# A product with 512 moving columns in place of two with 256, in six residual projections

## The chip, the cores and the metric

One Trainium2 chip, and one of its cores. The metric is the device time of one execution, in microseconds; the program is launched once and does the whole computation.

## The reference

Three blocks on one sequence of 256 tokens and 1024 features, in float32: a Mamba2 mixer with a conv FFN; differential attention with a conv FFN; and a block that joins a sparse attention and a gated recurrence, with a third conv FFN. What matters here is how each mixer and each FFN ends. It is a projection that is added to the stream `x`:

```python
x = x + y @ out_w                       # Mamba2, 2048 -> 1024       ("so")
x = x + (silu(gate) * up) @ down_w      # FFN, 2816 -> 1024          ("dn0", "dn1")
x = x + o @ attn_out_w                  # attention, 1024 -> 1024    ("ao")
h = h + ga1 * (merged @ w_out)          # 1024 -> 1024               ("wout")
h = h + ga2 * ((silu(gte) * val) @ w_down)   # 2816 -> 1024          ("dn2")
```

After each of them stands an RMS norm of the new `x` over its features, and the next products need its result.

## The kernel before

**Precision by halves.** Every large product is made from two halves of each operand. A weight slab (128 partitions x 2048 numbers, 1 MB) lands in `raw`; ScalarE rounds it to the float32r half `wh` (`split_hi`, line 377) and VectorE forms the rest `wl = raw - wh` (`split_lo`, line 384). Activations are split in the same way into a high and a low half. One contraction step is three matmuls of 128 x 128 weights and 256 moving columns (the tokens) into one PSUM bank (`mm3`, line 579): `wl*xh`, `wh*xl`, `wh*xh`. All of them are issued on line 584. I call the three a triple below.

**Streams.** `make_plan` (line 107) numbers all slabs, PSUM groups and semaphore counts in the order of the program. Slabs go through a ring of three buffers (`RING`) and PSUM groups through six banks (`PRING`). `stream` (line 587) waits for `lo_done` of a slab, takes a free bank for each output tile of 128 features and issues the triples. A 1 MB slab holds 16 triples: in `so` one tile of 16 steps, in `ao` and `wout` two tiles of 8 steps, in `dn` (kind `PAIR3`) three slabs of 16, 16 and 12 triples make two tiles of 22 steps each. So the six projections have 128, 176, 64, 176, 64 and 176 triples (so, dn0, ao, dn1, wout, dn2), 784 of the kernel's 2808.

**Who splits when.** There is no other scheduler than the written order of each engine's own queue. In a residual stage, at step s, VectorE (lines 1411 and 1430) does: one `ada` product, `split_lo` of slab s+2, a second `ada` product, and then for each tile m that is finished in step s the residual add (lines 1418, 1420, 1444, 1446), which gives the bank back, and `accumulate` of the square of tile m-1 (line 1380). ScalarE (lines 982 and 1008) does: `split_hi` of slab s+2, and then for each finished tile the square of the new `x[:, m]` (line 990), for which it waits until the bank has been given back. `split_hi` waits for the transfer of its slab and for TensorE to be through with the slab three before it. SyncE issues the load of a slab when `split_lo` of the slab three before it is done (line 516). ScalarE's last `split_hi` of a stage stands behind the square of tile 7 and ahead of the square root of the norm.

**The ada products.** The conditioning product `silu(c) @ w_ada` of the third block has no place of its own: VectorE works on it in 96 pieces of 128 x 512 numbers (`ada`, line 1358, instruction on line 1367), spread over the slabs of earlier streams by the table `ADA` (line 209): so 5 slabs, dn0 10, ao 3, dn1 10, with two pieces for each slab; wout and dn2 have none. The pieces come through a ring of two buffers (`ARING`) with 256 KB transfers that GpSimd issues (line 561), each after VectorE has used the piece two before it.

Of the kernel before, what the change touches and what calls it, by code (L numbers as in the profile page):

```python
# [236 lines left out]
def build_program(nc, io, out):  # L237
    with ExitStack() as ctx:
# [15 lines left out]
        xh = sb("xh", [P, KD, T], F32R)  # L254
        xl = sb("xl", [P, KD, T], F32R)
# [31 lines left out]
        def R(off, a, b):  # L287
            return actr[:, off:off + a * b].rearrange("p (a b) -> p a b", b=b)

# [111 lines left out]
        hh, hl = R(0, NF, T), R(NF * T, NF, T)  # L401
# [18 lines left out]
        yh, yl = R(0, 16, T), R(16 * T, 16, T)  # L420
# [14 lines left out]
        x2h, x2l = R(0, 8, T), R(8 * T, 8, T)  # L435
        oh, ol = R(16 * T, 8, T), R(24 * T, 8, T)
# [24 lines left out]
        rh, rl = R(0, 8, T), R(8 * T, 8, T)  # L461
        ah, al = R(16 * T, 4, T), R(20 * T, 4, T)
        mh, ml = R(24 * T, 8, T), R(32 * T, 8, T)
# [114 lines left out]
        def _(pe):  # L578
            def mm3(o, w, xp, start, stop, tok):

                (w_h, w_l), (x_h, x_l) = w, xp
                for n, (a, b) in enumerate(((w_l, x_h), (w_h, x_l), (w_h, x_h))):
                    l, r = (b, a) if tok else (a, b)
                    mm = nc.tensor.matmul(o, l, r, start=start and n == 0, stop=stop and n == 2)  # L584
                return mm

            def stream(name, X, ready=None):
# [6 lines left out]
                def stage(i, j):  # L594
# [4 lines left out]
                    if kind == TWO and ready and isinstance(i, int) and i == 0 and j == 0:  # L599
# [3 lines left out]
                        for k in range(kts):  # L603
                            ready(k)
                            for t in range(2):
                                off = k * width + t * P
                                mm = mm3(bank(g0 + t)[:, 0:T], (wh[:, r, off:off + P], wl[:, r, off:off + P]),
                                         (X[0][:, k, :], X[1][:, k, :]), k == 0, k == kts - 1, False)
                                if k == kts - 1:
                                    mm.then_inc(half_done if t == 0 else slab_done, 1)  # L610
                        return
                    for t in range(tiles):
# [14 lines left out]
                        for k in ks:  # L627
# [4 lines left out]
                            wp = (wh[:, r, off:off + P], wl[:, r, off:off + P])  # L632
                            mm = mm3(bank(g)[:, 0:T], wp, (X[0][:, k, :], X[1][:, k, :]), st, en, False)
# [7 lines left out]
            def stream_tok(name, X):  # L641

                for s in range(PL.N[name]):
# [3 lines left out]
                    for t in range(2):  # L647
                        g = PL.G[name] + 2 * s + t
                        acquire(pe, g)
                        for k in range(KD):  # L650
                            mm = mm3(bank(g)[:, 0:256],
                                     (wh[:, r, k * 256:k * 256 + 256], wl[:, r, k * 256:k * 256 + 256]),
                                     (X[0][:, k, P * t:P * t + P], X[1][:, k, P * t:P * t + P]),
                                     k == 0, k == KD - 1, True)
# [48 lines left out]
            stream("xbc", (xh, xl), x_ready(0))  # L703
# [58 lines left out]
            for gr in range(4):  # L762
                stream(f"za{gr}", (xh, xl))
# [8 lines left out]
                stream(f"zb{gr}", (xh, xl))  # L772
# [13 lines left out]
            stream("so", (yh, yl), lambda k: pe.wait_ge(low_done, k + 1))  # L786

            def ffn(f, norm, use, r):
                norm_sum(norm, r)
                stream(f"up{f}", (xh, xl), x_ready(use))  # L790
                stream(f"dn{f}", (hh, hl), lambda k: pe.wait_ge(low_done, LOW0 + NF * f + k + 1))
# [65 lines left out]
            for s in range(6):  # L857
                if s < 4:
                    stream(f"k{s}", (xh, xl), x_ready(2) if s == 0 else None)
# [6 lines left out]
                if s < 4:  # L866
                    stream(f"q{s}", (x2h, x2l), x_ready(3) if s == 0 else None)
                if 1 <= s < 5:
                    scores(2 * s - 1)
                if s < 4:  # L870
                    sums_by_token("kss", s, k_squares, halves)
                    stream_tok(f"v{s}", (xh, xl))
# [8 lines left out]
            stream("ao", (oh, ol), lambda k: pe.wait_ge(ol_done, k + 1))  # L881
# [12 lines left out]
            stream("qb", (xh, xl), x_ready(5))  # L894
            stream("kk", (xh, xl))
# [5 lines left out]
            for k in range(KD):  # L901
                o = k * 256
                mm = mm3(bank(g)[:, 0:T], (wh[:, b % RING, o:o + P], wl[:, b % RING, o:o + P]),
                         (xh[:, k, :], xl[:, k, :]), k == 0, k == KD - 1, False)
            mm.then_inc(half_done, 1)
            for c in range(2):
                for k in range(KD):
                    o = k * 256 + P
                    mm = mm3(bank(g + 1)[:, P * c:P * c + P], (wh[:, b % RING, o:o + P], wl[:, b % RING, o:o + P]),
                             (xh[:, k, P * c:P * c + P], xl[:, k, P * c:P * c + P]), k == 0, k == KD - 1, True)  # L910
            mm.then_inc(slab_done, 1)
            stream("qi", (xh, xl))
# [25 lines left out]
            for s in range(4):  # L938
                stream(f"yr{s}", (xh, xl))
                if s:  # L940
                    gates(s - 1)
                stream(f"xr{s}", (xh, xl))
            for it in range(9):
                if it < 8:
                    stream(f"{'ga' if it < 4 else 'gb'}{it%4}", (xh, xl))
# [20 lines left out]
            stream("woa", (ah, al), lambda k: pe.wait_ge(al_done, k + 1))  # L966
            pe.wait_ge(rl_done, 8)
            stream("wor", (rh, rl))
            stream("wout", (mh, ml), lambda k: pe.wait_ge(ml_done, k + 1))
# [377 lines left out]
        def _(dve):  # L1347
# [62 lines left out]

            def residual(name, r, n, tiles, scale=None):
                for s in range(n):
                    if s < n - 1:
                        lo(name, s)
                    for m, g, t, cnt in tiles(s):
                        wait_tile(dve, name, s // RING, s % RING, t, cnt)
                        if scale is None:
                            ins = V.tensor_tensor(x[:, m, :], bank(g)[:, 0:T], x[:, m, :], ALU.add)
                        else:
                            ins = V.scalar_tensor_tensor(x[:, m, :], bank(g)[:, 0:T], scale(m), x[:, m, :],  # L1420
# [695 lines left out]
```

## Time and profile before

| | |
|---|---|
| time, median of 3 runs | 1367.28 us (1366.11 to 1369.92) |
| span of the profiled execution, first to last instruction | 1370.0 us |
| TensorE (matmul) busy | 1218.9 us, 89% |
| VectorE busy | 936.6 us, 68% |
| ScalarE busy | 721.9 us, 53% |
| chain that ended last | PE 65%, DVE 15%, ACT 9%, DMA 6% |
| bytes read from HBM | 214.3 MB, 159 GB/s over the span |

The profile gives the span of its execution, not its device time; the span is 2.7 us over the median of the runs and 0.1 us over the slowest of them. The page names engines PE (TensorE), PEld (its weight loads), DVE (VectorE), ACT (ScalarE), POOL (GpSimd) and SP (SyncE). In a timeline, a row is one instruction or several alike that follow each other: start, time, engine, line, output<-inputs, shape, count, and in brackets how long the engine had been idle before it and what released it. Matmuls overlap, so what one costs in a dense stretch is the distance between starts and not its own duration.

### The profile page before, as it was taken

Reading aid. Unit: us, or ns where it says so; the run is one execution under the profiler, and the core shown is the slowest. Engines: PE = TensorE matmul, PEld = TensorE weight load, DVE = VectorE, ACT = ScalarE, POOL = GpSimd, SP = SyncE. Lnnn points to the kernel's source line nnn. Section 1 sums busy time; section 2 is a strip of 40 time slices with the busy share of each in tenths; the row PEclk is TensorE's granted clock in tenths of the full one; section 3 lists DMA queues with packets and bytes.
Section 4 is the critical chain, followed back from the end, with each engine's and each line's share of the span. In section 5 each row is a group of like instructions: output and inputs, shape, how many; then the busy total and the mean of one; then the engine's idle time right before and its main releaser. Section 6 shows DMA issues by size and latency. Waiting matters only on the chain.

```text
span 1370.0 us, 24509 instructions
## 1 busy us (share of the span) xinstructions
PE 1218.9 (89%) x9392; PEld 1183.2 (86%) x9392; DVE 936.6 (68%) x1699; ACT 721.9 (53%) x1078; POOL 56.6 (4%) x115
## 2 busy tenths in 40 slices
PE   4868989889999989886899999899777899999997
PEld 3868888889999988885899999898766788999997
DVE  4557778768787677665588877637865556888753
ACT  4354556446666336555366663446684434766641
POOL 1000000010000111010000001000000000000000
PEclk9988989999999999896899999889998989999998
DMA  6564422365554756442345557554322344455550
GB/s 236 126 186 154 133 99 100 129 233 181 181 181 163 261 200 223 139 144 80 139 158 183 183 177 265 186 185 133 130 93 78 123 154 154 158 182 183 175 192 32
DMA packets 38936, 219.62 MB, mean 160 GB/s; under 512 B 4775, under 2 KB 9160, under 8 KB 17352
## 3 DMA queue, kind: packets, MB, share of 16 engines
q1 hardware_dynamic: 26296, 185.83, 39.4%
q0 software_dynamic: 8112, 26.75, 5.6%
q10 hardware_dynamic: 4448, 5.94, 2.3%
q8 instruction: 55, 0.90, 0.3%
q14 instruction: 25, 0.20, 0.0%
HBM read 214.30 MB, written 4.19 MB: 159 GB/s over the span
## 4 chain that ended last, share of the span: by engine, by line
PE 65%; DVE 15%; ACT 9%; DMA 6%; issue 3%; ACTq 1%; SPq 0%; DVEq 0%
PE ps L584 58%; DMA raw<-in_xbc 4%; DVE wl L384 4%; ACT wh L377 3%; DMA ada_w<-in_w_ada 2%; PE ps L745 1%; DVE ada_w L1367 1%; DVE work L1399 1%; PE ps L671 1%; PE ps L756 1%; ACTq L1041 1%; DVE small L1743 1%; DVE work L1625 1%; DVE xl L1393 1%; DVE work L1874 1%
## 5 line engine op out<-in xcount | busy, mean ns | idle before, releaser
L584 PE MATMUL ps<-xh,wl 128*128 128x256 f32 x1784 | 520.0, 292 | 28.3 <-DVE wl L384 18.2
L584 PE MATMUL ps<-xl,wh 128*128 128x256 f32 x1784 | 515.0, 289 | 0.0
L584 PE MATMUL ps<-xh,wh 128*128 128x256 f32 x1784 | 514.4, 288 | 0.0
L384 DVE TENSOR_TENSOR wl<-raw,wh 128x2048 fp32r<-128x2048 f32 (+1 forms) x178 | 400.8, 2254 | 152.0 <-ACT wh L377 152.0
L584 PEld LDWEIGHTS ps<-xh,wl 128*128 128x128 f32 x1784 | 353.6, 198 | 34.2 <-DVE wl L384 19.1
L377 ACT ACTIVATE wh<-raw 128x2048 fp32r<-128x2048 f32 (+1 forms) x178 | 333.7, 1877 | 83.8 <-PE ps L584 55.2
L584 PEld LDWEIGHTS ps<-xl,wh 128*128 128x128 f32 x1784 | 353.3, 198 | 0.5 <-issue 0.2
L584 PEld LDWEIGHTS ps<-xh,wh 128*128 128x128 f32 x1784 | 353.0, 198 | 0.0
L584 PE MATMUL ps<-actr,wh 128*128 128x256 f32 x1888 | 342.8, 284 | 0.0
L584 PEld LDWEIGHTS ps<-actr,wh 128*128 128x128 f32 x1888 | 296.8, 193 | 0.1
L584 PE MATMUL ps<-actr,wl 128*128 128x256 f32 x944 | 270.2, 286 | 3.2 <-DVE wl L384 2.0
L584 PEld LDWEIGHTS ps<-actr,wl 128*128 128x128 f32 x944 | 182.7, 194 | 5.9 <-DVE wl L384 3.0
L1509 DVE SCALAR_TENSOR_TENSOR work<-ps,vecs,work 128x255 f32<-128x255 f32 (+1 forms) x336 | 143.8, 475 | 45.0 <-ACT work L1152 41.6
L1152 ACT ACTIVATE work<-ps,vecs 128x256 f32<-128x256 f32 x132 | 74.3, 565 | 140.9 <-PE ps L584 140.7
L990 ACT ACTIVATE work<-x 128x256 f32<-128x256 f32 x56 | 22.4, 416 | 132.2 <-DVE x L1444 37.6
L1367 DVE CUSTOM_DVE_ANT_0 ada_w<-ada_w,cact 128x512 f32<-128x512 f32 x96 | 65.3, 686 | 36.3 <-DMA ada_w<-in_w_ada 36.1
L561 POOL DMA_DIRECT2D ada_w<-in_w_ada x96 | 51.9, 541 | 814.8 <-DVE ada_sum L1367 814.0
L1185 ACT ACTIVATE work<-work,small 128x128 f32<-128x128 f32 (+1 forms) x48 | 21.5, 448 | 30.1 <-DVE small L1743 30.1
L1006 ACT ACTIVATE xh<-work 128x256 fp32r<-128x256 f32 x48 | 19.9, 417 | 19.0 <-DVE work L1399 18.5
L661 PEld LDWEIGHTS ps<-tri,work 128*128 128x128 f32 x60 | 9.9, 241 | 23.1 <-issue 23.1
L661 PE MATMUL ps<-tri,work 128*128 128x1 f32 x60 | 10.1, 282 | 22.1 <-DVE work L1380 22.1
L1143 ACT ACTIVATE work<-work 128x256 f32<-128x256 f32 x66 | 26.7, 404 | 2.9 <-DVE work L1509 2.8
(240 smaller groups left out, 1098.5 us busy)
## 6 DMA issues: line engine op xcount, KB each, us to landing
raw<-in_up SPq DMA_DIRECT2D x66, 1024.0 KB, 4.9
ada_w<-in_w_ada POOLq DMA_DIRECT2D x96, 256.0 KB, 4.4
raw<-in_xbc SPq DMA_DIRECT2D x12, 1024.0 KB, 16.1
raw<-in_z SPq DMA_DIRECT2D x8, 1024.0 KB, 4.9
raw<-in_so SPq DMA_DIRECT2D x8, 1024.0 KB, 5.1
raw<-in_dn0a SPq DMA_DIRECT2D x8, 1024.0 KB, 5.4
raw<-in_dn1a SPq DMA_DIRECT2D x8, 1024.0 KB, 5.3
raw<-in_dn2a SPq DMA_DIRECT2D x8, 1024.0 KB, 4.9
```

Source lines behind the costliest of these rows:

```text
L377: nc.scalar.activation(wh[:, b % RING, 0:n], raw[:, b % RING, 0:n], ACT.Copy).then_inc(hi_done, 1)
L384: nc.vector.tensor_tensor(wl[:, b % RING, 0:n], raw[:, b % RING, 0:n], wh[:, b % RING, 0:n].bitcast(F32), ALU.subtract).then_inc(lo_done, 1)
L561: pool.dma_start(ada_w[:, a % ARING, :], io["w_ada"][a // 2][:, 512 * (a % 2):512 * (a % 2) + 512])\
L584: mm = nc.tensor.matmul(o, l, r, start=start and n == 0, stop=stop and n == 2)
L661: mm = nc.tensor.matmul(o[:, n * b_:n * b_ + n], tile[:, P * b_:P * b_ + P], cols, start=True, stop=True)
L990: A(sq[:, m % 2, :], x[:, m, :], ACT.Square).then_inc(sq_done, 1)
L1006: A(xo[:, m, :], xn[:, m, :], ACT.Copy).then_inc(xh_done, 1)
L1143: A(gsil[:, (j - 1) % RING, :], pre[:, 2 * ((j - 1) % RING), :], ACT.Silu)\
L1152: A(pre[:, 2 * (j % RING) + t, :], bank(tile_group(up, j, t))[:, 0:T], ACT.Identity, scale=vdyn(f"up_w{f}", 88 + 2 * s + t), bias=vdyn(f"u ...
L1185: A(lg[:, cols], lg[:, cols], ACT.Exp, scale=-1.0, bias=mins[:, q, row + i:row + i + 1], accum_out=sums_[:, row + i:row + i + 1]).then_inc ...
L1367: V.tensor_tensor_reduce(out=w, in0=w, in1=cact[:, 512 * half:512 * half + 512], scale=1.0, scalar=0.0, op0=ALU.mult, op1=ALU.add, accum_o ...
L1509: return V.scalar_tensor_tensor(dst[:, d:T], src[:, 0:T - d], w, dst[:, d:T], ALU.mult, ALU.add)
```

## The change

The two halves of each operand become slices of one tensor, so that both halves of a moving tile can be named in one access (`xhl`, `yhl`, `hhl`, `ohl`, `mhl` and so on; the addresses inside are those of before). In the six residual projections the triple becomes two matmuls: `wh` against high and low half together, 512 moving columns, into both halves of the bank, and `wl` against the high half, 256 columns, into the first half of the bank. The residual then adds the two halves of the bank one after the other, with a wait on VectorE's own step counter between them. All other streams keep their three matmuls in the same order.

```diff
-        wh = sb("wh", [P, RING, SLOT], F32R)
-        wl = sb("wl", [P, RING, SLOT], F32R)
+        whl = sb("whl", [P, 2, RING, SLOT], F32R)
+        wh, wl = whl[:, 0, :, :], whl[:, 1, :, :]
...
+            def mm2(o, r, cols, X, k, start, stop):
+
+                nc.tensor.matmul(o, wh[:, r, cols], X[:, :, k, :], start=start, stop=False)
+                return nc.tensor.matmul(o[:, 0:T], wl[:, r, cols], X[:, 0, k, :], start=False, stop=stop)
...
-            def stream(name, X, ready=None):
+            def stream(name, X, ready=None, halved=False):
...
-                            wp = (wh[:, r, off:off + P], wl[:, r, off:off + P])
-                            mm = mm3(bank(g)[:, 0:T], wp, (X[0][:, k, :], X[1][:, k, :]), st, en, False)
+                            if halved:
+                                mm = mm2(bank(g), r, slice(off, off + P), X, k, st, en)
+                            else:
+                                mm = mm3(bank(g)[:, 0:T], r, slice(off, off + P), X, k, st, en)
...
-            stream("so", (yh, yl), lambda k: pe.wait_ge(low_done, k + 1))
+            stream("so", yhl, lambda k: pe.wait_ge(low_done, k + 1), halved=True)
...
-                stream(f"dn{f}", (hh, hl), lambda k: pe.wait_ge(low_done, LOW0 + NF * f + k + 1))
+                stream(f"dn{f}", hhl, lambda k: pe.wait_ge(low_done, LOW0 + NF * f + k + 1), halved=True)
...
-            stream("ao", (oh, ol), lambda k: pe.wait_ge(ol_done, k + 1))
+            stream("ao", ohl, lambda k: pe.wait_ge(ol_done, k + 1), halved=True)
...
-            stream("wout", (mh, ml), lambda k: pe.wait_ge(ml_done, k + 1))
+            stream("wout", mhl, lambda k: pe.wait_ge(ml_done, k + 1), halved=True)
...
+            def add_halves(m, g, scale):
+
+                for half in range(2):
+                    part = bank(g)[:, T * half:T * half + T]
+                    if half:
+                        step.wait()
+                    if scale is None:
+                        ins = V.tensor_tensor(x[:, m, :], part, x[:, m, :], ALU.add)
+                    else:
+                        ins = V.scalar_tensor_tensor(x[:, m, :], part, scale(m), x[:, m, :], ALU.mult, ALU.add)
+                    if half:
+                        give_back(ins, g)
+                    else:
+                        step.add(ins)
```

Both `residual` and `residual3` call `add_halves` where they had the one add.

## Rows read from the trace of the kernel before

**Rows 1.** The page, parts 1 and 4 (busy time; shares of the chain).
```profile
PE 1218.9 (89%) x9392; PEld 1183.2 (86%) x9392; DVE 936.6 (68%) x1699; ACT 721.9 (53%) x1078; POOL 56.6 (4%) x115
...
PE 65%; DVE 15%; ACT 9%; DMA 6%; issue 3%; ACTq 1%; SPq 0%; DVEq 0%
```

**Rows 2.** Busy time by window; columns PE, PEld, DVE, ACT, POOL, clock, DMA share, GB/s.
```profile
261.00:303.00 42.00, 39.93 (x326) 39.05 (x324) 28.51 (x55) 16.36 (x16) 5.38 (x10) 1.00 0.69 237
437.00:501.00 64.00, 63.63 (x531) 63.43 (x529) 43.04 (x72) 24.62 (x24) 10.76 (x20) 1.00 0.74 253
657.50:682.00 24.50, 24.27 (x193) 24.07 (x192) 16.27 (x31) 8.96 (x13) 3.23 (x6) 0.95 0.56 194
816.00:880.00 64.00, 63.37 (x529) 63.16 (x527) 43.15 (x72) 24.76 (x25) 9.68 (x18) 1.00 0.74 252
1137.00:1160.50 23.50, 22.91 (x191) 22.71 (x190) 14.63 (x24) 10.58 (x15) 0.00 (x0) 1.00 0.52 178
1296.00:1359.60 63.60, 63.04 (x526) 62.83 (x524) 28.37 (x30) 22.74 (x24) 0.00 (x0) 1.00 0.35 119
1200.00:1250.00 50.00, 50.00 (x419) 50.00 (x418) 40.30 (x60) 29.78 (x45) 0.00 (x0) 1.00 0.53 180
```

**Rows 3.** TensorE timeline: start, us, engine, line, instruction, count.
```profile
175.99 1.89 PE L725 MATMUL ps<-work,tri 128*128 128x256 f32 x8
...
657.67 0.63 PE L584 MATMUL ps<-actr,wh 128*128 128x256 f32 x2
...
917.80 0.28 PE L584 MATMUL ps<-wh,xl 128*128 128x128 f32 x1
...
918.81 0.27 PE L584 MATMUL ps<-wh,xl 128*128 128x128 f32 x1
```

**Rows 4.** The chain that ended last, end of so: start, us, what.
```profile
286.01 5.31 DMA ada_w<-in_w_ada
...
292.04 0.35 DVE x L1418
...
292.73 1.91 ACT wh L377
...
294.67 2.30 DVE wl L384
...
297.01 6.03 PE ps L584 x48
```

**Rows 5.** VectorE timeline: six dependent small instructions ahead of so; the last add of so.
```profile
261.30 1.18 DVE L1468 SCALAR_TENSOR_TENSOR small<-small 128x8 f32<-128x8 f32 x6
...
303.06 0.42 DVE L1418 TENSOR_TENSOR x<-ps,x 128x256 f32<-128x256 f32 x1 [0.53 <-PE ps L584]
```

**Rows 6.** VectorE timeline, ends of dn0 and dn1.
```profile
492.88 1.76 DVE L384 TENSOR_TENSOR wl<-raw,wh 128x1536 fp32r<-128x1536 f32 x1 [0.92 <-ACT wh L377]
...
500.67 0.42 DVE L1444 TENSOR_TENSOR x<-ps,x 128x256 f32<-128x256 f32 x1 [1.31 <-PE ps L584]
...
868.81 0.69 DVE L1367 CUSTOM_DVE_ANT_0 ada_w<-ada_w,cact 128x512 f32<-128x512 f32 x1 [3.40 <-DMA ada_w<-in_w_ada]
...
872.37 1.76 DVE L384 TENSOR_TENSOR wl<-raw,wh 128x1536 fp32r<-128x1536 f32 x1 [0.92 <-ACT wh L377]
...
879.40 0.42 DVE L1444 TENSOR_TENSOR x<-ps,x 128x256 f32<-128x256 f32 x1 [1.40 <-PE ps L584]
```

**Rows 7.** VectorE timeline, wout.
```profile
1153.86 2.29 DVE L384 TENSOR_TENSOR wl<-raw,wh 128x2048 fp32r<-128x2048 f32 x1 [1.71 <-ACT wh L377]
...
1159.95 0.48 DVE L1420 SCALAR_TENSOR_TENSOR x<-ps,small,x 128x256 f32<-128x256 f32 x1 [1.61 <-PE ps L584]
```

**Rows 8.** VectorE timeline, last two adds of ao; one split in dn2.
```profile
678.93 0.42 DVE L1418 TENSOR_TENSOR x<-ps,x 128x256 f32<-128x256 f32 x1 [1.22 <-PE ps L584]
...
681.81 0.42 DVE L1418 TENSOR_TENSOR x<-ps,x 128x256 f32<-128x256 f32 x1 [2.12 <-PE ps L584]
...
1325.09 2.29 DVE L384 TENSOR_TENSOR wl<-raw,wh 128x2048 fp32r<-128x2048 f32 x1 [3.47 <-ACT wh L377]
```

More of the change, by code:

```diff
@@ L288, in R, with RR @@
             return actr[:, off:off + a * b].rearrange("p (a b) -> p a b", b=b)
+        def RR(off, a, b):
+            return actr[:, off:off + 2 * a * b].rearrange("p (h a b) -> p h a b", h=2, b=b)
         KB = 256
@@ L578, in _, with mm3, mm3_tok @@
         def _(pe):
[L579 to L585, printed above, removed]
-            def stream(name, X, ready=None):
+            def mm3(o, r, cols, X, k, start, stop):
+                nc.tensor.matmul(o, wl[:, r, cols], X[:, 0, k, :], start=start, stop=False)
+                nc.tensor.matmul(o, wh[:, r, cols], X[:, 1, k, :], start=False, stop=False)
+                return nc.tensor.matmul(o, wh[:, r, cols], X[:, 0, k, :], start=False, stop=stop)
+            def mm2(o, r, cols, X, k, start, stop):
+                nc.tensor.matmul(o, wh[:, r, cols], X[:, :, k, :], start=start, stop=False)
+                return nc.tensor.matmul(o[:, 0:T], wl[:, r, cols], X[:, 0, k, :], start=False, stop=stop)
+            def mm3_tok(o, r, cols, X, k, toks, start, stop):
+                nc.tensor.matmul(o, X[:, 0, k, toks], wl[:, r, cols], start=start, stop=False)
+                nc.tensor.matmul(o, X[:, 1, k, toks], wh[:, r, cols], start=False, stop=False)
+                return nc.tensor.matmul(o, X[:, 0, k, toks], wh[:, r, cols], start=False, stop=stop)
+            def stream(name, X, ready=None, halved=False):
                 n, kind = PL.N[name], PL.kind[name]
@@ L606, in stage @@
                                 off = k * width + t * P
[L607 to L608 removed]
+                                cols = slice(off, off + P)
+                                if halved:
+                                    mm = mm2(bank(g0 + t), r, cols, X, k, k == 0, k == kts - 1)
+                                else:
+                                    mm = mm3(bank(g0 + t)[:, 0:T], r, cols, X, k, k == 0, k == kts - 1)
                                 if k == kts - 1:
@@ L1416, in residual @@
                         wait_tile(dve, name, s // RING, s % RING, t, cnt)
[L1417 to L1420, printed above, removed]
-                                                         ALU.mult, ALU.add)
-                        give_back(ins, g)
+                        add_halves(m, g, scale)
                         if m:
```

74 lines of the change are left out of this document (36 added, 38 removed).

## The prediction, made before the kernel with the change had run

> **What bounds the kernel now.** I read the shares first. TensorE's matmuls are busy 89% of the span and hold 65% of the chain that ended last [rows 1], so a change that takes time off matmuls looks right. But that is a mean over stages, and only six stages change. So the next view is the busy time of each of these [rows 2]: in dn0, dn1 and dn2 TensorE is busy over 99% of the window, in ao and wout 97 to 99%, in so 95%. Third, what a matmul costs: in a dense stretch 419 start in 50 us, one every 0.12 us, a triple in 0.36 us [rows 2], where the array needs 256 columns at 2.4 GHz, 0.107 us. Fourth, and this decides, for each stage the work that feeds TensorE and the work between its last matmul and the next stage: the chain and the timelines of VectorE [rows 4 to 8].
>
> **What a triple will cost.** Removed: one matmul of 256 columns and its weight load. Doubled: the columns of another. The trace has no float32r matmul of 512 columns. The nearest row is a float32 one of 256 columns, which shows as two records for each matmul and streams 512 array cycles in each: eight records in 1.89 us, the last lasting 0.38, so (1.89 - 0.38) / 7 = 0.216 us apart [rows 3]. That is 512 columns at 2.4 GHz (0.213) and almost nothing more, so the 0.013 us that today's matmul costs beyond its columns is not paid per column there. With half the columns (128) the distance is 0.112 (nine steps from 917.80 to 918.81) [rows 3]; so a floor near 0.11 per weight load holds short matmuls up, and a 512-column one covers it. I take 0.216 for the long one and leave 0.120 for the short one: 0.336 us for a triple in place of 0.360. Bounds: 0.360 if the long one costs twice 0.120, nothing gained; 0.325 if the short one falls to 0.109. Where the clock is at its lower level (1.2 GHz) matmuls stand 0.63 - 0.41 = 0.22 us apart [rows 3], which is all columns, and the change gives nothing; ao's mean clock of 0.95 over 24.5 us [rows 2] means 2.5 us at the lower level, its first four triples.
> The Trainium skill ("TensorE: Matmul & The Clock Gate", Back-to-back issue gap) gives a warm gap of N/2.4 + 2.5 ns: 109 for 256 columns, 216 for 512. By it a triple would cost 328 now and 325 after, and the change would have nothing to win. The long matmul's row agrees with it, the short one's (120) does not.
> At 24 ns for each of 784 triples the most to be had is 18.8 us: so 3.1, dn 4.2 each, ao and wout 1.5 each. What follows is how much of it each stage can use.
>
> **What the residual costs.** For each of 8 tiles in 6 stages VectorE runs a second add that waits for the first. An add takes 0.42 us (0.48 where it scales) [rows 6, 7], and a dependent instruction starts 0.03 us after its forerunner's end (six of 0.17 us in 1.18) [rows 5]. So each tile costs 0.45, in wout and dn2 0.51 us. The bank comes free that much later, and ScalarE's square waits for it; behind the square in ScalarE's queue stands the next `split_hi`, for which VectorE's `split_lo` waits, for which TensorE waits. Six banks cover the bank itself. Whether the loop is covered is a question for each stage. (The saved weight loads and the order `wh` before `wl` cost nothing, since both halves are there when `lo_done` lets TensorE start.)
>
> *so.* The chain does not run over matmuls here: it goes ada transfer (5.31 us), add, `split_hi`, `split_lo`, and TensorE starts the last slab at 297.01, right when its `split_lo` ends (294.67 + 2.30) [rows 4]. Faster matmuls are worth nothing, since each slab waits for its split. The extra adds are on this loop, except where an ada transfer hides one: tiles 1, 2 and 4, 3 x 0.45 = 1.35 us to the last slab. After it come tiles 5, 6 and 7 with one more `split_hi` and `split_lo` between them, another 1.35, less the 0.53 us for which VectorE waited for tile 7 [rows 5]. Sum: +2.2 us.
> *wout.* VectorE waits for `split_hi` before every split (1.71 us before the last), and only 1.61 us for TensorE before the last add [rows 7]. Loop: `split_hi`, `split_lo`, two tiles, square, next `split_hi`. Seven extra adds ahead of tile 7 are 3.6 us; the 1.61 us swallow part, tile 7's own second half comes on top: 8 x 0.51 - 1.6 = +2.4 us. TensorE is done 1.5 us earlier and waits.
> *ao.* The same loop, but VectorE waits 1.22 us for TensorE before tile 6 and 2.12 us before tile 7 [rows 8]: seven adds are 3.2, less 1.2 and some 0.4 at the first tiles, are +1.6 and stay under 2.12. Tile 7's first half starts 0.5 earlier (TensorE is through 1.5 earlier), its second costs 0.45: 0 to -0.2, I take -0.2 us. Price without that cover: +2.
> *dn2.* No ada products. VectorE sits idle 3.47 us before a split, for `split_hi`, which waits for TensorE [rows 8]: everything is fed early, a tile needs 22 triples and the adds fall beside them. 176 x 0.024 = 4.2 saved, tile 7's second half 0.51 exposed: -3.7 us.
> *dn0 and dn1.* TensorE looks just as full [rows 2], but the cover is nearly used up. dn1's last slab (36 matmuls, 4.3 us) starts at about 879.3 - 4.3 = 875.0, and its `split_lo` ends at 872.37 + 1.76 = 874.1: 0.9 us of slack; dn0: 500.6 - 4.3 = 496.3 against 494.64, 1.6 us [rows 6]. What delays the split is an ada piece: VectorE stood idle 3.40 us for its transfer at 868.81 [rows 6], then came two adds, squares, `split_hi`, `split_lo`. The DMA engines are at 0.74 with 252 GB/s in both stages, 0.35 and 119 in dn2 [rows 2]. Each transfer is issued when VectorE used the piece two earlier, so this is a loop of its own that a faster TensorE does not shorten. With the same transfers, the last split of dn1 comes 2 x 0.45 later (875.0) and the slab takes 4.0 instead of 4.3: end at 879.1, plus 0.45, is +0.3; dn0 in the same way -0.5. The adds of tiles 0 to 3 delay the issue of later pieces by up to 0.9 each time, partly hidden under transfers; I put +0.6 on each stage for it. dn0 +0.1, dn1 +0.9. Bounds for each: -3.7 (transfers never the limit) to +2.5 (every added pair lands on the loop).
>
> **Sum.** +2.2 + 2.4 - 0.2 - 3.7 + 0.1 + 0.9 = +1.7 us. The span was 1370.0 and the median of the runs is 1367.3, 2.7 us lower; I add the sum to the median: 1369.0 us. The runs before spread over 3.8 us, so what a measurement can tell from no change is about 0.3%, 4.1 us. A longer idle time between stages can also move where the clock falls and rises; I give it no price, the runs' spread contains it. The forecast is no measurable change: 18.8 us of matmul time saved on paper, one stage that cashes it.
>
> **Rivals.**
> 1. *The long matmul costs twice the short one* (0.240). For: no row shows float32r with 512 columns, and today's price is 0.013 over the columns in every dense stretch. Against: 0.216 in the float32 row. It decides in dn2, which then has +0.5 instead of -3.7; the others hardly move. Total +5.9, 1373.2 us: slower, by the second adds alone. Chance 0.13.
> 2. *The ada loop takes the adds in full.* In dn0 and dn1, at the add pairs of slabs 2, 5 and 8, each 0.9 us later issue of pieces, with none hidden: +2.5 for each stage. It decides from the point where a piece's landing after such a pair sets the next split, as at 868.81. Total +5.7, 1373.0 us. Chance 0.10.
> 3. *The ada loop gives way.* Slab loads start earlier with a faster TensorE and the pieces land in better gaps; for it speaks that DMA is at 0.74 and not full. Then dn0 and dn1 each give up to -3.7: total -6.7, 1360.6 us, faster. Against it: VectorE's idle time before pieces, up to 3.40 us [rows 6]. Chance 0.12.
> 4. *The short matmul gets cheaper behind a long one* (0.325 for a triple, the skill's gap for both): only dn2 can use it, 176 x 0.011 = 1.9 more, total -0.2, 1367.1 us. Chance 0.15.
> The forecast itself has 0.50; about 0.05 of that lies beyond 0.3% on the slow side and 0.01 on the fast one.
>
> **Numbers.** Faster: rival 3 without its weaker half and the forecast's edge, 0.12. Slower: rivals 1 and 2 and the edge, 0.28. Same: 0.60. The range holds the forecast, rival 4 and all but the ends of the others: 1362.5 to 1374.
>
> **What would show it.** dn2: 176 triples in 59.1 us instead of 63.4, its last add 3.7 us earlier against its first matmul. so and wout: TensorE idle before slabs on `wl`, and VectorE no longer waiting for TensorE ahead of the last add. dn1: TensorE waits for `split_lo` of its last slab. Wrong would be: long matmuls not 0.216 apart; so or wout no longer than before; dn0 and dn1 each 3 us shorter.

## The result and the profile after

The kernel with the change took 1377.4 us (median of 5 runs, 1371.94 to 1379.46), the kernel before, measured beside it, 1366.11 (1365.31 to 1369.92). The ratio is 1.0067, with a 95% interval of 1.0049 to 1.0085: **some 9 us slower** (the two medians stand 11.3 apart), where no change was forecast (1369.0 us, range 1362.5 to 1374.0). The profiled execution took 1378.39 us, its span is 1376.7, 6.7 more than the span before. The span is 1.7 us less than the time of its own execution, so the execution traced before took about 1371.7 us (an estimate), more than any run of its table; the two spans therefore differ by less than the times.

The page after, its first line, the busy shares, the shares of the chain, and one of its groups (out<-in, count, busy us, mean ns, idle time before):

```profile
span 1376.7 us, 22989 instructions
...
PE 1212.3 (88%) x8608; PEld 1137.3 (83%) x8608; DVE 956.6 (69%) x1747; ACT 722.3 (52%) x1078; POOL 56.4 (4%) x115
...
PE 52%; DVE 21%; ACT 12%; DMA 9%; issue 5%; ACTq 1%; SPq 0%; DVEq 0%
...
L1009 ACT ACTIVATE work<-x 128x256 f32<-128x256 f32 x56 | 23.2, 417 | 154.1 <-DVE x L1437 85.2
```

784 matmuls are gone (9392 to 8608), and TensorE's share of the chain falls from 65% [rows 1] to 52%, while VectorE, ScalarE and DMA take 42% in place of 30%. What ends late now is what feeds TensorE. Line 1437 holds the pair of adds of a tile (line 1439 where they scale); ScalarE's squares (L1009) spend 85.2 us of their waiting on L1437, where it was 71.7 us on the single adds of the same stages (37.6 on L1444 and 34.1 on L1418). The same six stages by window, in the order of [rows 2] without its last row:

```profile
260.70:302.70 42.00, 37.25 (x204) 30.80 (x202) 30.53 (x51) 14.38 (x15) 5.37 (x10) 1.00 0.65 223
436.40:500.40 64.00, 61.74 (x351) 53.30 (x350) 44.95 (x77) 24.28 (x23) 10.73 (x20) 1.00 0.71 243
657.60:682.10 24.50, 23.54 (x129) 20.26 (x128) 19.37 (x39) 9.15 (x13) 3.22 (x6) 0.95 0.56 186
816.10:880.10 64.00, 61.15 (x342) 52.57 (x341) 43.93 (x74) 24.16 (x23) 9.66 (x18) 0.99 0.68 235
1140.50:1164.00 23.50, 22.57 (x128) 19.31 (x126) 15.93 (x26) 9.83 (x12) 0.00 (x0) 1.00 0.43 143
1302.20:1365.80 63.60, 62.23 (x353) 53.72 (x351) 32.65 (x39) 23.40 (x24) 0.00 (x0) 1.00 0.36 120
...
877.20:882.00 4.80, 4.80 (x19) 4.15 (x20) 3.93 (x6) 0.42 (x1) 0.00 (x0) 0.65 0.80 261
```

TensorE was busy for 39.93 of 42 us in so, now for 37.25; in dn1 63.37 of 64, now 61.15. The last row is the last slab of dn1: a mean granted clock of 0.65, so most of it at the lower level (1.2 GHz), where [rows 2] have 1.00 for all of dn1.

**By stage.** From the TensorE timelines of both traces, each stage from its first matmul to the next stage's first (dn2: to its last add):

```
stage   before   after   difference   forecast
so       56.6     58.0      +1.4        +2.2 (with 0.5 more in up0's first slabs: +1.9)
dn0      69.5     70.7      +1.2        +0.1
ao       30.4     30.4       0.0        -0.2
dn1      79.3     83.5      +4.2        +0.9
wout     29.3     32.2      +3.0        +2.4
dn2      64.0     63.4      -0.65       -3.7
```

With +1.9 for so they sum to +9.7. The other stretches, whose code is the same, came out 3.0 shorter in this one execution, 2.6 of them ahead of so. From so's first matmul to the end it took 1117.6 us before and 1126.9 after, 9.3 more, which is what the ratio says (9.2).

One of those stretches is longer: the norm behind dn2, with its small matmuls (L661 and L671 before, L681 and L691 after). TensorE at the end of the kernel, before, then after:

```profile
1360.62 0.58 PE L661 MATMUL ps<-tri,work 128*128 128x1 f32 x4 [1.58 <-DVE work L1380]
1361.84 0.68 PE L671 MATMUL ps<-ident,small 128*128 128x128 f32 x4 [0.64 <-DVE small L1386]
...
1366.53 0.82 PE L681 MATMUL ps<-tri,work 128*128 128x1 f32 x4 [2.10 <-DVE work L1399]
1367.99 1.19 PE L691 MATMUL ps<-ident,small 128*128 128x128 f32 x4 [0.64 <-DVE small L1405]
```

TensorE has been idle for 2.10 us in place of 1.58, and the mean granted clock of the norm is 0.66 (1365.5 to 1369.2) instead of 1.00 (1359.6 to 1362.6). From dn2's last add to the end it took 11.20 us and not 10.44, so the 0.65 that dn2 saved is gone again. In wout the last add came 2.5 us later after the stage's first matmul (26.19 us against 23.72), and the other 0.5 of its +3.0 is the norm again: its second group took 1.19 us instead of 0.68. Such a half microsecond needs no change, though: the trace of the kernel before without the ada pieces (below) has it behind wout, too, and behind dn0 the norm came out 0.5 shorter with the change (5.00 against 5.51 from the last add to the next slab). The 0.75 behind dn2 stands in both profiles of the change and in none of the kernel before.

**The long matmul.** TensorE's timeline in dn2, start, us, instruction (answers to [rows 3]):

```profile
1355.08 0.40 PE L595 MATMUL ps<-actr,whl 128*128 128x512 f32 x1
1355.31 0.28 PE L596 MATMUL ps<-actr,whl 128*128 128x256 f32 x1
1355.43 0.40 PE L595 MATMUL ps<-actr,whl 128*128 128x512 f32 x1
...
1359.67 0.40 PE L595 MATMUL ps<-actr,whl 128*128 128x512 f32 x1
```

Twelve triples in 4.24 us, so 0.353 each (forecast 0.336, before 0.360): over all of dn2 the long matmul stands 0.236 ahead of the short one and not 0.216, and the short one 0.117 ahead of the next long one. 784 triples save 5.3 us on paper instead of 18.8.

**so and wout.** ScalarE and VectorE at the end of so, then of wout (answers to [rows 4, 5, 7]; in brackets the idle time before and what ended it):

```profile
294.98 0.88 DVE L1437 TENSOR_TENSOR x<-ps,x 128x256 f32<-128x256 f32 x2
...
295.89 0.42 ACT L1009 ACTIVATE work<-x 128x256 f32<-128x256 f32 x1 [3.15 <-DVE x L1437]
296.21 1.90 ACT L381 ACTIVATE whl<-raw 128x2048 fp32r<-128x2048 f32 x1
298.15 2.29 DVE L388 TENSOR_TENSOR whl<-raw,whl 128x2048 fp32r<-128x2048 f32 x1 [1.96 <-ACT whl L381]
...
1157.29 0.42 ACT L1009 ACTIVATE work<-x 128x256 f32<-128x256 f32 x1 [0.44 <-DVE x L1439]
1157.61 1.90 ACT L381 ACTIVATE whl<-raw 128x2048 fp32r<-128x2048 f32 x1
1159.55 2.29 DVE L388 TENSOR_TENSOR whl<-raw,whl 128x2048 fp32r<-128x2048 f32 x1 [1.96 <-ACT whl L381]
1161.76 1.00 DVE L1439 SCALAR_TENSOR_TENSOR x<-ps,small,x 128x256 f32<-128x256 f32 x2
```

This is the loop of the prediction: two adds (0.88, or 1.00 where they scale), the square, only then `split_hi`, for which VectorE waits 1.96 us, then `split_lo`. In wout VectorE waited 1.61 us for TensorE before the last add [rows 7]; now nothing stands there but the adds themselves.

**dn1.** The chain that ended last, through the end of dn1 (start, us, what):

```profile
860.31 4.41 DMA ada_w<-in_w_ada
...
865.74 5.12 DMA ada_w<-in_w_ada
...
870.89 0.69 DVE ada_w L1386
...
873.09 0.44 DVE x L1437
...
873.55 0.02 ACT work L1009
...
873.87 1.48 ACT whl L381
...
875.38 1.77 DVE whl L388
...
881.29 0.21 PE ps L596
881.51 0.43 PE ps L595
```

In [rows 6] the piece before dn1's last split was taken at 868.81, 53.0 us after the stage's first matmul; now it is 870.89, 54.9 us. Behind it come two tiles' adds, two squares, `split_hi` and `split_lo`. TensorE's timeline around the start of the last slab:

```profile
874.59 0.28 PE L596 MATMUL ps<-actr,whl 128*128 128x256 f32 x1
877.19 0.50 PE L595 MATMUL ps<-actr,whl 128*128 128x512 f32 x1 [2.33 <-DVE whl L388]
```

It idles 2.33 us, and then its pairs stand 0.64 us apart (0.21 + 0.43, the chain's last two lines; 768 columns at 1.2 GHz) instead of 0.353: the last slab takes 5.73 us to its last matmul, 1.6 more than twelve triples take at the full clock (4.12).

**dn0, ao, dn2** (VectorE, answers to [rows 6, 8]):

```profile
490.51 0.69 DVE L1386 CUSTOM_DVE_ANT_0 ada_w<-ada_w,cact 128x512 f32<-128x512 f32 x1 [4.25 <-DMA ada_w<-in_w_ada]
...
681.46 0.88 DVE L1437 TENSOR_TENSOR x<-ps,x 128x256 f32<-128x256 f32 x2
...
1364.47 1.00 DVE L1439 SCALAR_TENSOR_TENSOR x<-ps,small,x 128x256 f32<-128x256 f32 x2 [0.78 <-PE ps L596]
```

dn0 waits for a piece as dn1 does. In ao the last pair of adds follows without a wait: the 2.12 us of [rows 8] are used up, and no more than that. In dn2 the last pair takes 0.52 more than the single add did.

### The profile page after: what moved, and what is told of

The parts are those of the page before. It is cut to its first block, busy times and chain, and to the rows that moved or that the text cites. A ratio compares the mean times of both kernels' runs of the same rounds, so it can differ in the third digit from the quotient of the medians.

```text
span 1376.7 us, 22989 instructions
## 1 busy us (share of the span) xinstructions
PE 1212.3 (88%) x8608; PEld 1137.3 (83%) x8608; DVE 956.6 (69%) x1747; ACT 722.3 (52%) x1078; POOL 56.4 (4%) x115
## 4 chain that ended last, share of the span: by engine, by line
PE 52%; DVE 21%; ACT 12%; DMA 9%; issue 5%; ACTq 1%; SPq 0%; DVEq 0%
PE ps L589 13%; PE ps L591 13%; PE ps L590 13%; DVE whl L388 6%; DMA ada_w<-in_w_ada 5%; ACT whl L381 5%; PE ps L595 5%; DMA raw<-in_xbc 4%; PE ps L596 2%; DVE ada_w L1386 2%; DVE x L1437 1%; DVE work L1418 1%; PE ps L691 1%; PE ps L765 1%; PE ps L776 1%
## 5 line engine op out<-in xcount | busy, mean ns | idle before, releaser
L589 PE MATMUL ps<-xhl,whl 128*128 128x256 f32 x1784 | 519.6, 291 | 29.7 <-DVE whl L388 19.6
L590 PE MATMUL ps<-xhl,whl 128*128 128x256 f32 x1784 | 514.2, 288 | 0.0
L591 PE MATMUL ps<-xhl,whl 128*128 128x256 f32 x1784 | 513.8, 288 | 0.0
L388 DVE TENSOR_TENSOR whl<-raw,whl 128x2048 fp32r<-128x2048 f32 (+1 forms) x178 | 400.9, 2254 | 151.2 <-ACT whl L381 151.1
L589 PEld LDWEIGHTS ps<-xhl,whl 128*128 128x128 f32 x1784 | 353.2, 198 | 35.7 <-DVE whl L388 20.6
L381 ACT ACTIVATE whl<-raw 128x2048 fp32r<-128x2048 f32 (+1 forms) x178 | 333.3, 1877 | 69.5 <-PE ps L596 27.8
L590 PEld LDWEIGHTS ps<-xhl,whl 128*128 128x128 f32 x1784 | 352.9, 198 | 0.5 <-issue 0.2
L591 PEld LDWEIGHTS ps<-xhl,whl 128*128 128x128 f32 x1784 | 352.1, 197 | 0.0
L595 PE MATMUL ps<-actr,whl 128*128 128x512 f32 x784 | 281.4, 403 | 8.4 <-DVE whl L388 8.0
L596 PE MATMUL ps<-actr,whl 128*128 128x256 f32 x784 | 221.0, 282 | 0.0
L595 PEld LDWEIGHTS ps<-actr,whl 128*128 128x128 f32 x784 | 148.9, 190 | 48.2 <-DVE whl L388 11.0
L596 PEld LDWEIGHTS ps<-actr,whl 128*128 128x128 f32 x784 | 149.5, 191 | 0.1
L1009 ACT ACTIVATE work<-x 128x256 f32<-128x256 f32 x56 | 23.2, 417 | 154.1 <-DVE x L1437 85.2
L589 PE MATMUL ps<-actr,whl 128*128 128x256 f32 x160 | 46.4, 290 | 1.2 <-DVE actr L1412 1.2
L590 PE MATMUL ps<-actr,whl 128*128 128x256 f32 x160 | 45.8, 286 | 0.0
L591 PE MATMUL ps<-actr,whl 128*128 128x256 f32 x160 | 45.8, 286 | 0.0
L681 PE MATMUL ps<-tri,work 128*128 128x1 f32 x60 | 10.9, 295 | 27.7 <-DVE work L1399 27.7
```

Source lines behind the costliest of these rows:

```text
L381: nc.scalar.activation(wh[:, b % RING, 0:n], raw[:, b % RING, 0:n], ACT.Copy).then_inc(hi_done, 1)
L388: nc.vector.tensor_tensor(wl[:, b % RING, 0:n], raw[:, b % RING, 0:n], wh[:, b % RING, 0:n].bitcast(F32), ALU.subtract).then_inc(lo_done, 1)
L589: nc.tensor.matmul(o, wl[:, r, cols], X[:, 0, k, :], start=start, stop=False)
L590: nc.tensor.matmul(o, wh[:, r, cols], X[:, 1, k, :], start=False, stop=False)
L591: return nc.tensor.matmul(o, wh[:, r, cols], X[:, 0, k, :], start=False, stop=stop)
L595: nc.tensor.matmul(o, wh[:, r, cols], X[:, :, k, :], start=start, stop=False)
```

## The experiments

Each ratio is to the kernel before, run beside it on the same chip (medians of 1367.7 to 1368.6 us there), with its 95% interval.

### The two halves of the change, each alone

```
# e1: matmuls of the change, one add       # e2: three matmuls of 256, two adds
-  for half in range(2):                   -  mm = mm2(bank(g), ...)
+  for half in (1,):                       +  mm = mm3(bank(g)[:, 0:T], ...)
+    part = bank(g)[:, 0:T]                +    part = bank(g)[:, 0:T]   # both times
     ...                                        ...
```

> The matmuls of the change, but a single add for each tile (it takes the first half of the bank; the second half, the product with the low part of the activations, is left out of the result). Theory A (two causes add up: a triple saves only 0.007 us instead of 0.024, and the second adds sit on a loop over VectorE and ScalarE in so, wout, dn0 and dn1): without the second adds the kernel is faster than before by what dn2, dn1, dn0 and ao can use of 0.007 us for each triple, 1 to 4 us: 1362 to 1365 us. Theory B (the matmuls themselves do the harm: TensorE is through earlier, waits, and its clock falls after the idle time, as in the last slab of dn1): 1368 us or more, and dn1's last slab again takes 5.7 us.

Measured: 1366.3 us, ratio 0.9981 (0.9966 to 0.9995). Theory A expected 1 to 4 us less than before, and the matmuls alone do help, by 2.6 us (its 1362 to 1365 us are missed, since the kernel before ran at 1368.6 here). But stage by stage it is not smooth: dn2 gives -1.2, so -1.2, dn1 -1.7 (the stretch behind it, up to wout, came out 1.6 longer), and dn0 loses 3.7. The execution traced was the slowest of the ten, 1369.82 us, so the loss in dn0 may well be larger than in most. The timeline of VectorE and TensorE at the end of dn0:

```profile
488.34 0.69 DVE L1386 CUSTOM_DVE_ANT_0 ada_w<-ada_w,cact 128x512 f32<-128x512 f32 x1 [4.56 <-DMA ada_w<-in_w_ada]
...
493.71 0.50 PE L595 MATMUL ps<-actr,whl 128*128 128x512 f32 x1 [2.83 <-DVE whl L388]
```

and the window of its last slab (columns as in [rows 2]):

```profile
493.00:500.00 7.00, 6.01 (x24) 4.94 (x24) 4.47 (x7) 1.09 (x2) 0.54 (x1) 0.76 0.89 317
```

VectorE idle for 4.56 us ahead of a piece, TensorE for 2.83, then a clock of 0.76: what happened in dn1 with the change happens in dn0 without a single added add. Theory B is right about one thing, the clock fell behind this wait, but the matmuls are not the loss: with them alone the kernel is faster.

> The three matmuls of 256 columns as before the change, with the change's two adds for each tile (both take the first half of the bank, so the stage's result is added twice). Theory A: so +2.2, wout +3.5, dn0 +1.3, dn1 +2.5 to +4, ao +0.5, dn2 +0.5: 10.5 to 12 us over the kernel before, 1376.5 to 1378.5 us, about the time of the change itself. Theory B (matmuls and the clock do it): half of that or less, 1367 to 1372 us.

Measured: 1376.76 us, ratio 1.0062 (1.0038 to 1.0085): nearly all of the change's 1.0067. By stage: so +1.7 and up0's first slabs +0.4, dn0 +1.9, ao +0.6, wout +3.0, dn1 -0.1. So the adds are the loss; the saved matmuls give little of it back. It is 8.5 us over the kernel before, less than theory A's 10.5 to 12. For dn1 theory A said +2.5 to +4, and this execution shows nothing there; up1 and the stretch behind dn1, up to wout, whose code is the same, were 1.4 longer each. The two halves add up to 5.9 us and the change to 9.2; with intervals of 2 to 3 us on each of the three, that gap isn't clear of the noise.

### Without the ada pieces of dn0 and dn1

```
-  ..., "so": 5, "dn0": 10, ... "ao": 3, "dn1": 10}
+  ..., "so": 5,            ... "ao": 3}
-  for a in range(96):       # POOL issues the pieces
+  for a in range(56):
```

> The change, without the 40 ada pieces of dn0 and dn1 (their transfers and products are left out, and so the modulation of the second block is incomplete). Theory A (in dn0 and dn1 the adds land on the loop of the ada pieces): both stages then behave like dn2, each 0.7 us shorter than the same stage of the kernel before without those pieces; the difference to that kernel is then so +2, wout +3, dn2 -0.7, dn0 -0.7, dn1 -0.7, ao 0: +3 us. Theory C (dn0 and dn1 lose for another reason, such as VectorE's own work or the clock): the difference to that kernel stays at 8 to 11 us.

> The kernel before without the same 40 ada pieces: the base for the run above. TensorE is busy over 99% of dn0 and dn1 there, so both theories expect little: 0 to -2 us against the kernel before, 1364 to 1366 us.

Measured: 1.0023 (1.0009 to 1.0037) for the change and 0.9992 (0.9975 to 1.0008) for the kernel before, both without the pieces: 0.31% apart, 4.2 us, where with the pieces it is 9.2. Between the two traces dn0 differs by -0.8, dn1 by -0.7, dn2 by -1.2 to its last matmul (-0.65 to its last add), so by +3.1, wout by +2.5. The stretches behind dn0 (up to ao) and behind dn1 (up to wout) differ by +0.9 and +0.6, so it isn't clear that what dn0 and dn1 save reaches the end. In dn1 of the change without pieces VectorE waits for TensorE before the adds of tile 6:

```profile
873.40 0.88 DVE L1437 TENSOR_TENSOR x<-ps,x 128x256 f32<-128x256 f32 x2 [3.48 <-PE ps L596]
```

With the pieces gone, TensorE never waits there and the change is no loss in any of the three dn stages. That is theory A's result, and 8 to 11 us (theory C) did not come. The run takes away the products on VectorE as well as the transfers, 20 of 0.69 us in each stage, so it doesn't tell these two apart by itself; that it is the transfer is read from VectorE's idle time for it before the last split (4.25 us in dn0 with the change, 4.56 in the run above). The pieces cost the kernel before nothing that its times show.

### The price of the long matmul

Ten groups of matmuls behind the kernel's last one (`cols(i)` stands for a block of 128 columns that changes with each i), as

```
+  for i in range(32):
+      nc.tensor.matmul(pt[:, 0, :], whl[:, 0, i % 2, cols(i)], xhl[:, :, i % 6, :], ...)
+      nc.tensor.matmul(pt[:, 0, 0:T], whl[:, 1, i % 2, cols(i)], xhl[:, 0, i % 6, :], ...)
```

> The change with ten groups of matmuls put behind its last one, into two banks that nothing reads: 96 and 64 of 256 columns; 32 long ones (512 columns) whose two halves lie 8 KB apart; 32 long ones of 512 adjacent columns; then pairs of a long and a short one: halves 8 KB apart, 22 KB apart, adjacent, and with the short one in the other bank; the three of 256; and 16 times each long-short-short and long-long-short. Theory P (every matmul pays some 0.011 us beyond its columns, long or short, and the pair pays once less than the triple): long alone 0.225 apart, a pair 0.345 to 0.353, the same for halves 8 KB, 22 KB apart and adjacent. Theory Q (a long one from two separate runs of columns pays for the jump between them): adjacent columns give 0.216 for the long one and 0.336 for the pair, separate ones 0.235 and 0.353. Theory R (the long one pays for its columns twice what the short one pays, 0.240, and the short one is cheaper behind it): long alone 0.240 wherever its columns lie.

The run took 1478.69 us; the added matmuls fill the last 108 of them, the first ones still at the lower clock. The timeline of TensorE (L995 short alone, L997 long alone with separate halves, L999 long alone with adjacent columns, L1004 pairs with the halves 22 KB apart, L1007 pairs with adjacent columns; of pairs the long one's lines):

```profile
1384.84 0.88 PE L995 MATMUL pt<-xhl,whl 128*128 128x256 f32 x6
...
1389.82 1.52 PE L997 MATMUL pt<-xhl,whl 128*128 128x512 f32 x6
...
1396.62 1.98 PE L999 MATMUL pt<-xhl,whl 128*128 128x512 f32 x8
...
1415.68 0.40 PE L1004 MATMUL pt<-actr,whl 128*128 128x512 f32 x1
...
1418.15 0.40 PE L1004 MATMUL pt<-actr,whl 128*128 128x512 f32 x1
...
1426.63 0.40 PE L1007 MATMUL pt<-xhl,whl 128*128 128x512 f32 x1
...
1429.10 0.40 PE L1007 MATMUL pt<-xhl,whl 128*128 128x512 f32 x1
```

Short: (0.88 - 0.28) / 5 = 0.120 apart. Long: (1.52 - 0.39) / 5 = 0.226, adjacent (1.98 - 0.39) / 7 = 0.227. Seven pairs from 1415.68 to 1418.15 and from 1426.63 to 1429.10: 0.353 each in both; the pairs with halves 8 KB apart and those with the short one in another bank have it too. So where the columns lie makes no difference (theory Q falls), and the long one is not twice the short one (R falls). Theory P is nearest: 512 columns at 2.4 GHz are 0.213, 256 are 0.107, and both cost 0.013 more. A pair would be 0.346 by that; it is 0.353. Over whole groups the triple of short ones takes 0.360, as before; long-short-short 0.468, nearly the sum of its parts (0.226 + 2 x 0.120 = 0.466); long-long-short 0.585, 0.013 more than its parts (0.572). Why a pair costs 0.007 more than its parts is not explained.

### ScalarE's split ahead of the squares

```
 def residual(name, r, n, last_of):
+    hi(name, 0)
     for s in range(n):
-        if s < n - 1:
-            hi(name, s)
+        if s + 1 < n - 1:
+            hi(name, s + 1)
         for m, g in last_of(s):
             square(r, m, g)
```

> The change, with ScalarE's next `split_hi` moved ahead of the squares of the tile before it, in all six stages. Theory A (the second adds cost so and wout time because the next `split_hi` stands behind the square, which waits for both adds): so and wout get back what they lost and some of what the kernel before already spent there: so -2 to -4, wout -3 to -5, dn0 and dn1 -0 to -4, against the change: 5 to 9 us below it, 1367 to 1371 us. Theory D (VectorE's own queue is the limit: two adds, an accumulation and the split for each slab): less than 2 us below the change.

> The kernel before with the same move of `split_hi`. Theory A: so -1 to -2, wout -1 to -2 (it waits less, TensorE was nearly full there), 1364 to 1366 us; so the move is worth more to the change than to the kernel before, and the two end within 3 us of each other. Theory D: no difference, 1367 to 1369 us.

Measured: 1367.49 us, 0.9993 (0.9983 to 1.0004) for the change and 0.9988 (0.9973 to 1.0002) for the kernel before; again, in more rounds:

> The kernel before with `split_hi` ahead of the squares, again, in more rounds and on one chip with the three above: 0.9988 of the kernel before (0.9975 to 0.9995).

0.9991 (0.9980 to 1.0003), as expected. The move gives the change its 9 us back; for the kernel before the times show 1.2 to 1.6 us, with intervals that just reach 1, and the two traces -1.8 us in so. With the move the change loses nothing in so (-1.6 against the kernel before, where that one with the move has -1.8), 0.6 instead of 3.0 in wout; of that 0.6 the last add is 0.1, the rest the norm at the lower clock. The kernel before gained nothing in wout by the move, where theory A had put -1 to -2. ScalarE and VectorE in wout of the change with the move:

```profile
1142.31 1.92 ACT L381 ACTIVATE whl<-raw 128x2048 fp32r<-128x2048 f32 x1 [0.91 <-PE ps L596]
...
1153.55 1.00 DVE L1440 SCALAR_TENSOR_TENSOR x<-ps,small,x 128x256 f32<-128x256 f32 x2 [1.48 <-PE ps L596]
```

`split_hi` now waits for TensorE alone, and the adds run beside it; before the last pair VectorE waits for TensorE again (1.48). Theory D falls: VectorE has time for the second adds, as long as nothing stands behind them.

### VectorE's split ahead of the ada pieces

```
 def lo(name, s):
-    ada(name, s)
     split_lo(dve, PL.S[name] + s + LEAD)
     ada(name, s)
+    ada(name, s)
```

> The change, with VectorE's `split_lo` ahead of both ada pieces of its slab in place of between them (in every stage with pieces). Theory A (in dn0 and dn1 the last slab's split stands behind a piece whose transfer is late): dn1 -3 to -4 us and dn0 -1 us against the change, so gains too, since its last split stands behind a piece as well (up to -2): 4 to 7 us below the change, 1370 to 1373 us. Theory E (what delays the last split is `split_hi` behind the adds and squares, the pieces lie beside it): less than 1.5 us below the change.

Measured: 1391.05 us, 1.0155 (1.0127 to 1.0184) of the kernel before, by the two ratios 12 us *slower* than the change (1.0067). Both theories missed. VectorE, and the issues on POOL, in dn1:

```profile
858.31 0.69 DVE L1386 CUSTOM_DVE_ANT_0 ada_w<-ada_w,cact 128x512 f32<-128x512 f32 x1 [2.67 <-DMA ada_w<-in_w_ada]
...
858.96 0.69 DVE L1386 CUSTOM_DVE_ANT_0 ada_w<-ada_w,cact 128x512 f32<-128x512 f32 x1
859.31 1.18 POOL L569 DMA_DIRECT2D ada_w<-in_w_ada  x2 [5.04 <-DVE ada_sum L1386]
...
859.58 2.29 DVE L388 TENSOR_TENSOR whl<-raw,whl 128x2048 fp32r<-128x2048 f32 x1
863.33 0.69 DVE L1386 CUSTOM_DVE_ANT_0 ada_w<-ada_w,cact 128x512 f32<-128x512 f32 x1 [1.47 <-DMA ada_w<-in_w_ada]
```

There are two buffers. With both pieces used back to back, both are free at the same time, both transfers go out together (x2), and VectorE stands idle for each pair. Pieces on either side of a split leave each transfer half a slab more. This shows the loop from the other side: in dn0 and dn1 the time from the use of a piece to the landing of the next in its buffer is what paces VectorE. Against the kernel before dn0 lost 5.5 us, dn1 5.2, and the stretch between dn0 and ao, which has pieces too, 4.0.

### The change again, and versions that use the wide matmul in fewer stages

> The change once more, nothing edited, for a second profile of it. Theory A: so (with the start of up0) +1.5 to +2.5, wout +3, dn2 -1.2, the same as in its first profile, since each of their slabs waits for the same splits; dn0 and dn1 may come out anywhere from -1.2 to +4 each, depending on whether the last slab's split waits for an ada piece for 1 us or for 3. Whole: 1.004 to 1.008 times the kernel before. If so or wout differ by over 1 us between the two profiles, the account by stages is not to be trusted.

Measured: 1.0074 (1.0055 to 1.0094). Between its trace and that of before: so and up0's first slabs +2.0, wout +3.0, dn2 -1.2 to its last matmul (-0.65 to its last add), as expected; dn0 +2.3, dn1 +4.35. From so's first matmul to the end it is +10.0. By TensorE's timeline dn0's last slab waited 1.79 us for its split, then took 5.73 us; in the change's first profile it had waited 2.26 and took 4.15. `h1_matmul_bench` has the change's own code up to the end of dn2, so its trace is a third profile of that part: dn0 +2.2 (a wait of 2.13 us, then 4.15 us for the slab), dn1 only +1.2 (a wait of 1.31, then 4.22). Of the eight waits of 1.8 us or more before a last slab in dn0 or dn1 (two in this profile and two in the change's first, one in `h1`, one in `e1`, and 3.01 and 3.83 us in `k3`) six were followed by a slab of 5.71 to 5.75 us; the two that were not are 2.13 and 2.26 us. How long the wait was does not decide it alone.

```
+ halved = name in ("dn0", "dn1", "dn2", "ao")     # m2: name in ("dn2",)
```

> The wide matmul and its second add in dn0, dn1, dn2 and ao alone; so and wout as in the kernel before; `split_hi` moved ahead of the squares in all six. Theory A: so and wout as in the kernel before with the early split (0 to -1.5 us), dn2's matmuls -1.2 and its second add +0.5, dn0 and dn1 -1 to +1 each: 1 to 2 us below the kernel before with the early split, 0.997 to 0.998 of the kernel before. Rival: the ada loop takes what dn0 and dn1 save, and the result is that of the early split alone (0.9988).

> The same, with the wide matmul in dn2 alone, the one stage without ada pieces and with its splits ahead. Theory A: 0.7 us below the kernel before with the early split, too little to be told from it by the times (0.998 to 0.9985 of the kernel before), visible in the trace as dn2's last slab 1.2 us earlier.

Measured: 0.9994 (0.9979 to 1.0010) with four stages, 0.9986 (0.9973 to 0.9999) with dn2 alone; the early split without any wide matmul had 0.9991 beside them. The three can't be told apart. Against the trace of the early split alone, four stages give dn0 -1.0, dn1 -0.1, ao -0.3, dn2 -1.2 to its last matmul, but +0.9 in the stretch behind dn0 and +0.5 behind wout's last add: the 1 to 2 us that theory A had put below the early split did not come. dn2 alone gives -1.17 to its last matmul and nothing anywhere else, which is 176 triples by 0.0067; to its last add 0.65 of it is left. Of these three the version with dn2 alone is the only one whose interval lies below 1, by less than 2 us.

## Why the prediction was wrong, step by step

**Right.** *so* (+2.2 forecast, +1.9), *wout* (+2.4, and its last add came 2.5 later) and *ao* (-0.2, 0.0): read from who waits for whom behind the square, and shown by the move of `split_hi`, which takes these losses away. The price of an added add, 0.45 and 0.51 us, is what the pairs show (0.88 for two against 0.42, 1.00 against 0.48). That the saved matmul time is worth nothing in so isn't shown: with the matmuls alone so came out 1.2 shorter, but without the pieces of dn0 and dn1, which changes nothing in so, the kernel before had it 1.0 shorter as well. In wout 1.61 us of VectorE's waiting were to swallow part of the adds, and they did. Two details were off there: TensorE is through 0.4 us earlier and not 1.5, and it is never idle ahead of a slab of wout. The 0.5 us by which the stage as a whole came out above that is the norm at the lower clock.

**Wrong: the long matmul, "I take 0.216".** It measured 0.236 ahead of a short one (0.226 alone). The row it was taken from, float32 of 256 columns in two records each, showed almost no cost beyond the columns; float32r pays 0.013 for a long matmul as for a short one, and the change between both another 0.007. So the 0.013 is not a floor of the weight load that 512 columns cover, as the prediction argued from the 128-column rows. A triple is 0.353 and not 0.336. The term was *dn2*, -3.7: it became -0.65, 3.0 us of the miss. Rival 1 named this term, with 0.240 and +0.5 for dn2; the truth lies between, nearer to it, though the long one alone is not twice the short one. The formula of the Trainium skill that was weighed there ("TensorE: Matmul & The Clock Gate", Back-to-back issue gap) puts the long one at 216 ns. The trace disagrees (236), as it did for the short one (120 against 109); but what follows from it, a triple that saves 3 ns, was closer to the 7 measured than the forecast's 24.

**Wrong: "I put +0.6 on each stage for it"**, the later issue of ada pieces in *dn0 and dn1*. The piece ahead of dn1's last split came 54.9 us into the stage and not 53.0: 2.0 us, over three times the 0.6. The second term, 0.9 for the two pairs of adds behind it, was right, and so, nearly, was the slack of 0.9, which the two used up. What had no term is what came behind TensorE's idle time of 2.33 us: a last slab with a granted clock of 0.65 over 4.8 us, 1.6 us more. Put together, 0.3 with 2.0 in place of 0.6, with 0.1 for a slab of 4.12 and not 4.0, and with 1.6 for the clock make 4.0 of the 4.2. The text said that "a longer idle time between stages can also move where the clock falls and rises; I give it no price": it fell inside a stage, and in the norm behind dn2 as well (+0.75). Rival 2 named this loop, with a bound of +2.5 for each stage; dn1 took +4.2, +4.35 and +1.2 in three profiles, dn0 +1.2, +2.3 and +2.2. The bound was too low for the first two because it priced the adds alone.

**The sum.** -3.7 to -0.65 is +3.0, dn0 +1.1, dn1 +3.3, wout +0.6, ao +0.2, so -0.3: 7.9 us over +1.7, which makes +9.7. The sum had no term for the 0.75 behind dn2's last add, either; the stretches behind dn0 and dn1 gave 1.1 back in this trace. Two rivals that were weighed one at a time, 0.13 and 0.10, came together, each in part, and each had been given a total in which the other did not happen; the range ended where either alone ended.

**What stays open.** How dn0 and dn1 share their loss between faster matmuls and later adds: with the matmuls alone dn0 lost 3.7 and dn1 gained 1.7, with the adds alone dn0 lost 1.9 and dn1 nothing, one profile each. Why the clock fell after six of eight such waits is open, too. Shown is that without the ada pieces there is no loss, that each half of the change can by itself bring a wait in dn0 (2.83 us with the matmuls alone, before the last slab; 1.16 with the adds alone, earlier in the stage), and that moving `split_hi` ahead of the squares takes it away (dn0 0.0, dn1 -0.7). A third buffer for the pieces wasn't tried.

## What to carry to other kernels

Merging two matmuls that share weights saves at most what a matmul costs beyond its columns (13 ns here, of which 7 in 360 were left), and not the columns; measure that in a few rows of the very dtype and width before planning on it. An operation added at a tile's end costs what stands behind it in every queue: here a split behind a square behind the add, and moving that split ahead was worth as much as the whole change cost. And where a slack of under a microsecond is used up by two terms at once, price what comes after the wait as well, in the norm behind a stage too.

## What the runs showed of the hardware that was not expected

- A float32r matmul costs 13 ns beyond its columns whether it has 256 or 512 of them, adjacent or in two runs 8 or 22 KB apart (0.120, 0.226); in a strict long-short change the pair costs 0.353 and not 0.346.
- After six of eight waits of 1.8 to 3.8 us inside dn0 and dn1 the next slab ran for most of it at the clock's lower level (slabs of 5.71 to 5.75 us instead of 4.12 to 4.2, mean granted clock 0.71); after the other two, of 2.13 and 2.26 us, the clock stayed at 1.00. After four waits of 1.1 to 1.3 us (second profile of the change, `h1`, `e2`, `k3`) it stayed at 1.00 as well.
- The second group of small matmuls of a norm took 1.19 us where the granted clock was at its lower level and 0.68 where it was not; behind dn2's last add that and the first group made 0.75 us.
- One piece of 256 KB took 4.41 and 5.12 us from issue to landing in dn1, while the DMA engines were at a share of 0.78 (860.3 to 870.9), so the two-buffer loop was the limit there and the engines were not full.
